# Dilated attention in a two-block kernel: exponentials by each key set's own maximum, weighed together at the division

## What is computed

```python
for q, k, v, off in zip(qs, ks, vs, offs):          # three sets
    s = einsum('bqhd,bqkhd->bhqk', qi, kg) * scale  # masked: -inf outside
    lse = logsumexp(s); p = exp(s - lse)
    outs.append(einsum('bhqk,bqkhd->bqhd', p, vg)); lses.append(lse)
wts = softmax(stack(lses), axis=0)
return sum(wts * stack(outs), axis=0)
```

## Time and profile before

| | |
|---|---|
| median of 3 runs | 1580.39 us (1578.71 to 1582.65) |
| the profiled execution's own time | 1575.34 us |
| its span in the trace | 1573.4 us |
| TensorE busy | 1500.6 us (95%) |
| VectorE busy | 924.0 us (59%) |
| ScalarE busy | 627.8 us (40%) |
| granted TensorE clock, mean | 0.974 of full speed |

### The profile page before, as it was taken

The page is one execution under the profiler, slowest core; times in us unless marked ns, Lnnn a source line. Parts: engine busy times, 40 slices in busy tenths (PEclk is TensorE's granted clock), DMA queues, the critical chain, the costliest instruction groups (busy, mean ns, idle before and its releaser), DMA issues.

```text
span 1573.4 us, 20863 instructions
## 1 busy us (share of the span) xinstructions
PE 1500.6 (95%) x8538; PEld 1112.7 (71%) x8538; DVE 924.0 (59%) x1573; ACT 627.8 (40%) x1018; POOL 39.8 (3%) x39
## 2 busy tenths in 40 slices
PE   7999999998999999998799999999999999999998
PEld 6876343336988534433678778989987877889897
DVE  4975111118896411112998778988868856765555
ACT  6442111114333211112554655444445556454443
POOL 0000000000000000000400000000001000000000
PEclk9999999998999999999899999999999999999999
DMA  9877999995564999999646243998935522435540
GB/s 358 315 308 304 411 421 421 422 421 223 205 269 170 402 410 420 422 421 419 227 164 241 108 149 148 351 344 320 361 117 195 193 96 83 159 136 186 188 161 27
DMA packets 58777, 420.77 MB, mean 267 GB/s; under 512 B 6625, under 2 KB 6689, under 8 KB 8370
## 3 DMA queue, kind: packets, MB, share of 16 engines
q1 hardware_dynamic: 58034, 417.19, 68.0%
q0 software_dynamic: 640, 2.14, 0.4%
HBM read 418.26 MB, written 1.05 MB: 266 GB/s over the span
## 4 chain that ended last, share of the span: by engine, by line
PE 80%; DVE 12%; ACT 6%; DMA 1%; issue 1%; SPq 0%; DVEq 0%; ACTq 0%
PE ps L758 77%; DVE lo L1874 3%; ACT AR L1775 3%; DVE AR L1867 2%; PE ps L844 1%; DMA raw<-in_moe 1%; ACT hi L1444 1%; DVE ACC L1867 1%; DVE AR L1864 1%; PE ps L1328 1%; PE ps L1067 1%; PE ps L1302 1%; ACT AR L1787 0%; DVE TINY L1867 0%; DVE TINY L1864 0%
## 5 line engine op out<-in xcount | busy, mean ns | idle before, releaser
L1874 DVE TENSOR_TENSOR lo<-raw,hi 128x1024 fp32r<-128x1024 f32 x300 | 367.3, 1246 | 106.4 <-ACT hi L1444 105.4
L1444 ACT ACTIVATE hi<-raw 128x1024 fp32r<-128x1024 f32 x300 | 310.4, 1056 | 194.7 <-PE ps L758 189.3
L758 PE MATMUL ps<-T,hi 128*128 128x256 f32 x1792 | 333.1, 287 | 8.8 <-DVE lo L1874 8.5
L758 PEld LDWEIGHTS ps<-T,hi 128*128 128x128 f32 x1792 | 284.5, 194 | 20.2 <-DVE lo L1874 9.3
L758 PE MATMUL ps<-hi,T 128*128 128x512 f32 x896 | 286.7, 396 | 3.9 <-DVE T L1867 3.0
L758 PE MATMUL ps<-T,lo 128*128 128x256 f32 x896 | 255.2, 285 | 0.0
L758 PEld LDWEIGHTS ps<-hi,T 128*128 128x128 f32 x896 | 169.9, 190 | 40.7 <-issue 5.7
L758 PE MATMUL ps<-lo,T 128*128 128x512 f32 x448 | 175.6, 392 | 0.0
L758 PEld LDWEIGHTS ps<-T,lo 128*128 128x128 f32 x896 | 173.5, 194 | 0.0
L758 PE MATMUL ps<-hi,AF 128*128 128x512 f32 x512 | 166.1, 396 | 0.5 <-DVE AF L2593 0.5
L1867 DVE SCALAR_TENSOR_TENSOR AR<-AR,ps 128x512 f32<-128x512 f32 x52 | 35.6, 686 | 179.6 <-ACT AR L1605 110.9
(11 more groups left out here) (234 smaller groups left out, 1819.8 us busy)
## 6 DMA issues: line engine op xcount, KB each, us to landing
raw<-in_moe SPq DMA_DIRECT2D x76, 1024.0 KB, 16.7
raw<-in_b_ff SPq DMA_DIRECT2D x64, 1024.0 KB, 5.1
AR<-in_moe SPq DMA_DIRECT2D x60, 1024.0 KB, 15.4
raw<-in_ada SPq DMA_DIRECT2D x48, 1024.0 KB, 6.6
ring<-in_moe SPq DMA_DIRECT2D x44, 1024.0 KB, 15.8
raw<-in_b_in SPq DMA_DIRECT2D x24, 1024.0 KB, 6.5
raw<-in_b_gate SPq DMA_DIRECT2D x16, 1024.0 KB, 4.8
ACC<-in_moe SPq DMA_DIRECT2D x12, 1024.0 KB, 18.5
```

Source lines behind the costliest of these rows:

```text
L758: return e.matmul(o, l, r, start=a, stop=z, skip_group_check=True)
L1444: e.activation(hi[n % NC][:, :], raw[place[c]][:, 1024 * half:1024 * half + 1024], ACT.Copy).then_inc(*to("hi", "hi", n))
L1874: tt(lo[n % NC][:, :], r, hi[n % NC][:, :], SUB).then_inc(*to("lo", "lo", n))
```

## The change

Each b set now gets its own exponentials by its own maximum as soon as that is known. After the third set VectorE takes the largest of the three maxima and each set's distance to it (`off`, six numbers for a query row); ScalarE turns these into weights (`part`). At the division VectorE multiplies sums by weights, adds, takes the reciprocal and multiplies weights by it, and each set is scaled by its own factor. The division becomes a job of its own, "soft", that is yielded with the score job of the next pair; after the last pair it takes a yield of its own, so that what follows it (probs 7 onward) moves by one yield: value 6 comes after `bb` tile 1 instead of tile 0, value 7 after tile 2, value 8 after tile 3, ahead of value 9.

```diff
             if j < PAIRS:
-                yield [("score", j)]
+                yield [("score", j)] + ([("soft", j - 1)] if j else [])
+            elif j == PAIRS:
+                yield [("soft", j - 1)]
...
+        def soft_mem(i):
+            return tuple(tiny(f"b_{x}{i % 4}", 6) for x in ("le", "of", "pa", "sm"))
...  ScalarE, job "score"
                             i, n, of, _, _, _, g = SETS[j]
-                            if n < of - 1:
-                                continue
-                            mx, sm = tiny(f"b_mx{i % 2}", 8), tiny(f"b_sm{i % 2}", 8)
-                            w.wait_ge(*after("max", l, i))
-                            for k in range(of):
-                                jj = j - 2 * (of - 1 - k)
-                                [waits for probs jj - 8, or for qk_turn]
-                                for q in range(2):
-                                    [exp of PB[jj % 8][:, q, :], bias mx[:, q], sum to sm[:, 2 + 2 * k + q]]
+                            less, off, part, sm = soft_mem(i)
+                            if n == 2:
+                                w.wait_ge(*after("off", l, i))
+                                e.activation(part, off, ACT.Exp, scale=m.SC).then_inc(*to("tile_out", "part", l, i))
+                            w.wait_ge(*after("max", l, j))
+                            [waits for probs j - 8, or for qk_turn]
+                            for q in range(2):
+                                [exp of PB[j % 8][:, q, :], bias less[:, 2 * n + q], sum to sm[:, 2 * n + q]]
...  VectorE, largest(j)
-                        if n < 2:
-                            return
-                        w.wait_ge(*last("step"))
-                        e.tensor_reduce(mx[:, 0:2], mx[:, 2:8].rearrange("p (g q) -> p q g", q=2), AX.X, MAX).then_inc(*to("step"))
                     w.wait_ge(*last("step"))
-                    ts(mx[:, 0:2], mx[:, 0:2], -m.SC, None, MUL, NOP).then_inc(*to("step", "max", l, i))
+                    ts(less[:, x], most[:, x], -m.SC, None, MUL, NOP).then_inc(*to("step", "max", l, j))
+                    if n == 2:
+                        e.tensor_reduce(most[:, 6:8], most[:, 0:6].rearrange("p (g q) -> p q g", q=2), AX.X, MAX).then_inc(*to("step"))
+                        w.wait_ge(*last("step"))
+                        tt(off.rearrange("p (g q) -> p g q", q=2), most[:, 0:6].rearrange("p (g q) -> p g q", q=2),
+                           most[:, 6:8].unsqueeze(1).broadcast_to([128, 3, 2]), SUB).then_inc(*to("step", "off", l, i))
...  VectorE, divided(j), b heads
-                        e.tensor_reduce(sm[:, 0:2], sm[:, 2:8].rearrange("p (g q) -> p q g", q=2), AX.X, ADD).then_inc(*to("step"))
-                        w.wait_ge(*last("step"))
-                        e.reciprocal(sm[:, 0:2], sm[:, 0:2]).then_inc(*to("step"))
+                        w.wait_ge(*after("part", l, i))
+                        tt(by, sm, part, MUL).then_inc(*to("step"))
+                        w.wait_ge(*last("step"))
+                        e.tensor_reduce(total[:, 0:2], by.rearrange("p (g q) -> p q g", q=2), AX.X, ADD).then_inc(*to("step"))
+                        w.wait_ge(*last("step"))
+                        e.reciprocal(total[:, 2:4], total[:, 0:2]).then_inc(*to("step"))
+                        w.wait_ge(*last("step"))
+                        tt(by.rearrange("p (g q) -> p g q", q=2), part.rearrange("p (g q) -> p g q", q=2),
+                           total[:, 2:4].unsqueeze(1).broadcast_to([128, 3, 2]), MUL).then_inc(*to("step"))
                     w.wait_ge(*last("step"))
                     for k in range(of):
                         jj = j - 2 * (of - 1 - k)
                         for q in range(2):
-                            o = m.PB[jj % 8][:, q, :]
-                            ins = ts(o, o, sm[:, q:q + 1], None, MUL, NOP)
+                            o, x = m.PB[jj % 8][:, q, :], 2 * k + q
+                            ins = ts(o, o, by[:, x:x + 1], None, MUL, NOP)
...  VectorE, the walk
                     elif what == "score":
                         for j in (2 * a[0], 2 * a[0] + 1):
                             largest(j)
+                    elif what == "soft":
                         for j in (2 * a[0], 2 * a[0] + 1):
                             divided(j)
```

More of the change, by code:

```diff
@@ L1761, in attention @@
                             i, n, of, _, _, _, g = SETS[j]
-                            if n < of - 1:
-                                continue
-                            mx, sm = tiny(f"b_mx{i % 2}", 8), tiny(f"b_sm{i % 2}", 8)
-                            w.wait_ge(*after("max", l, i))
-                            for k in range(of):
-                                jj = j - 2 * (of - 1 - k)
[L1768 to L1771, removed]
-                                for q in range(2):
-                                    o = m.PB[jj % 8][:, q, :]
-                                    src = PS[bank["score", l, j]][:, 256 * q:256 * q + 256] if g is None else o
-                                    ins = e.activation(o, src, ACT.Exp, scale=m.SC, bias=mx[:, q:q + 1],
-                                                       accum_out=sm[:, 2 + 2 * k + q:3 + 2 * k + q])
+                            less, off, part, sm = soft_mem(i)
@@ new lines, in attention @@
+                            if n == 2:
+                                w.wait_ge(*after("off", l, i))
+                                e.activation(part, off, ACT.Exp, scale=m.SC).then_inc(*to("tile_out", "part", l, i))
+                            w.wait_ge(*after("max", l, j))
+                            if j > 7:
+                                w.wait_ge(*after("probs", l, j - 8))
+                            else:
+                                w.wait_ge(*after("qk_turn", l, 5, 0))
+                            for q in range(2):
+                                o, x = m.PB[j % 8][:, q, :], 2 * n + q
+                                src = PS[bank["score", l, j]][:, 256 * q:256 * q + 256] if g is None else o
+                                ins = e.activation(o, src, ACT.Exp, scale=m.SC, bias=less[:, x:x + 1], accum_out=sm[:, x:x + 1])
@@ L1777, in attention @@
                             if g is None:
                                 ins.then_inc(*to("tile_out", "score_out", l, j))
-                                also(("exp", l, i), ("score_out", l, j))
+                                also(("exp", l, j), ("score_out", l, j))
                             else:
-                                ins.then_inc(*to("tile_out", "exp", l, i))
+                                ins.then_inc(*to("tile_out", "exp", l, j))
                     elif what == "probs":
@@ L2457, in largest @@
                 def largest(j):
-                    i, n, of, qp, kp, _, g = SETS[j]
-                    mx = tiny(f"b_mx{i % 2}", 8)
+                    i, n, of, _, _, _, g = SETS[j]
+                    most, x = tiny(f"b_mx{i % 4}", 8), slice(2 * n, 2 * n + 2)
+                    less, off, _, _ = soft_mem(i)
                     pb, p = m.PB[j % 8], PS[bank["score", l, j]]
@@ L2463, in largest @@
                     if g is None:
-                        e.tensor_reduce(mx[:, 0:2], p[:, :].rearrange("p (q k) -> p q k", q=2), AX.X, MAX).then_inc(*to("step"))
+                        e.tensor_reduce(most[:, 0:2], p[:, :].rearrange("p (q k) -> p q k", q=2), AX.X, MAX).then_inc(*to("step"))
                     else:
@@ L2473, in largest @@
                                                          m.MK[:, g, 256 * q:256 * q + 256], 1.0, -3e38, ADD, MAX,
-                                                         mx[:, 2 + 2 * n + q:3 + 2 * n + q])
+                                                         most[:, 2 * n + q:2 * n + q + 1])
                         ins.then_inc(*to("step", "score_out", l, j))
-                        if n < 2:
-                            return
+                    w.wait_ge(*last("step"))
+                    ts(less[:, x], most[:, x], -m.SC, None, MUL, NOP).then_inc(*to("step", "max", l, j))
+                    if n == 2:
+                        e.tensor_reduce(most[:, 6:8], most[:, 0:6].rearrange("p (g q) -> p q g", q=2), AX.X, MAX).then_inc(*to("step"))
                         w.wait_ge(*last("step"))
-                        e.tensor_reduce(mx[:, 0:2], mx[:, 2:8].rearrange("p (g q) -> p q g", q=2), AX.X, MAX).then_inc(*to("step"))
-                    w.wait_ge(*last("step"))
-                    ts(mx[:, 0:2], mx[:, 0:2], -m.SC, None, MUL, NOP).then_inc(*to("step", "max", l, i))
+                        tt(off.rearrange("p (g q) -> p g q", q=2), most[:, 0:6].rearrange("p (g q) -> p g q", q=2),
+                           most[:, 6:8].unsqueeze(1).broadcast_to([128, 3, 2]), SUB).then_inc(*to("step", "off", l, i))
                 def divided(j):
@@ L2486, in divided @@
                         return
-                    sm = tiny(f"b_sm{i % 2}", 8)
```

(12 more changed lines are left out.)

## The result

The changed kernel takes 1590.27 us in the median of 9 runs (1587.40 to 1597.21), the kernel before beside it 1581.22 (1576.77 to 1586.58, 9 runs). The ratio is 1.0064, with a 95% interval of 1.0047 to 1.0081: about 10.1 us slower, by the ends 7.4 to 12.8. Forecast were +6.4 us, 1586.8 us, and 1582 to 1591. The direction and the places were as forecast, and the median lies within the forecast range; the loss itself was underpriced, by 2.7 us by the medians and 3.7 by the ratio. What follows finds the rest in TensorE's clock: about half of the loss is waiting and about half is work at half clock.

The account below looks back on a forecast made before the run. TensorE was taken as the bound (80% of the span), so only its stalls counted: 2.2 + 5.8 - 1.6 = +6.4 us, clock 0, on 1580.39 gave 1586.8 us. The range for 8 in 10 was 1582.0 to 1591.0.

Parts of the forecast that it names:

- Place A: At probs 0 and 1, divisions ready later for TensorE: 0.5 us lost in layer 0, 1.7 in layer 1, +2.2.
- Place B: Before probs 3, second b division queued behind `lo` and score 6's maxima: new stall, 2.9 us a layer, +5.8.
- Place C: At the first `bb` tile, work arrives 0.8 us earlier; stall falls from 3.48 to 2.7, -1.6 for two layers.
- Prices: Trace-based costs: small instructions 0.20 us apart with a wait, 0.07 without; division chain 0.8; `part` 0.2, bounds 0 to 0.5.
- The queue ledger of 6.4 us: Sum over the three places in both layers: 2.2 + 5.8 - 1.6 = +6.4 us.
- The rule of the Trainium skill: Chained VectorE instructions cost the same with and without a semaphore; as a rival +2.5 us, 1582.9, chance 0.05.
- Clock: TensorE's half-speed stretches after stalls, some 1.6 us each: gain and loss counted equal, 0, ends -3.2 and +3.2.
- The low rival: No slow stretch after the `bb` 0 stall or the new one before probs 3: +3.2 us, 1583.6; chance 0.20.
- The "not slower" rival: Exponentials alone held the division at probs 0; maxima and late `lo` fit idle time: -7.5 us, 1572.9; chance 0.06.
- The dearer rival: Low clock at all three places and `part` at its upper bound: +10.8 us, 1591.2; chance 0.10.

Follow-up runs that it names:

- the filled kernels: The kernel before and the changed kernel, each with throw-away transposes filling TensorE's stalls; 1574.71 us and 1578.98 us.
- own_same_job: Changed kernel with each division back in the job of its own pair and without the last division's extra yield; 1579.14 us, ratio 0.9991.
- delay_only: Kernel before with only the divisions a pair later, maxima still joint and exponentials where they were; 1597.38 us, ratio 1.0094.
- after_again: The changed kernel run once more, unchanged; 1591.83 us, ratio 1.0067.
- heads_filled: Like own_same_filled, with 16, 3 and 20 filling transposes and the first set of both heads multiplied first; 1576.78 us, ratio 0.9973.
- own_same_filled: own_same_job with filling transposes: 16 before tile 0's, 13 before tile 1's, 24 before the first `bb` matmul; 1572.82 us, ratio 0.9952.
- after_filled: Changed kernel with throw-away transposes before tiles 0, 1, 6, 7 and `bb` 0 (26, 6, 4, 10, 18); 1578.98 us, ratio 0.9979.

## Why the prediction was right and wrong

**Right.** *Place A*, 0.5 and 1.7 us: from score 0 to the transposes of tile 1 the filled kernels differ by 0.6 us in layer 0 and 1.8 in layer 1. Late `hi` behind early exponentials showed as `lo` waiting for ScalarE, 0.16 us in layer 0 where `ada` covers it. *Place B*, 2.9 a layer: 0.84 and 1.65, taken away by own_same_job, made larger by delay_only. That the user of the division doesn't move with it was the main term, and it is shown. *Place C*, -0.8 a layer: 3.48 to 2.71. *Prices*: small waiting instructions 0.20 apart, chain 0.79, `part` 0.21. The queue ledger of 6.4 us came out as 2.6 and 3.9 up to `bb` 0 with the clock held. The rule of the Trainium skill ("VectorE: DVE Perf Modes", The DRAIN you can't avoid) on semaphores between chained instructions, which would have given +2.5, doesn't hold for instructions of 2 to 6 numbers a partition in the rows before and after: they start 0.20 apart with a wait and 0.07 without, and four with waits take 0.79.

**Wrong.** The step that failed is **Clock**, "So I count the gain and the loss as equal, 0." The term was about +6 as a sum of lost time, and about +5 net of what hides in the stalls. Busy time at half clock loses half of itself (2.88 x 0.5 = 1.4 over 868 to 871). Added up in this way over the windows, the profiled execution before loses 3.3 us behind A and 3.2 behind C, 6.5 in all. The one after loses 5.9 behind A (3.7 and 2.2 in the two layers), 4.8 behind B (1.7 and 3.1) and 1.7 behind C, 12.4 in all. So A gave +2.7 where the prediction had 0. B gave +4.8, of which it had allowed for 3.2 at most, and C gave -1.5, where it had hoped for up to -3.2. In the second execution, after_again, the sum is 13.3. The fillers give the two numbers another way: 5.9 and 11.3 us are won back. Two things had been missed. The low stretch behind A was longer, 6.8 or 10.2 us in all four layers profiled and not 3.4. The longer stall there may be the cause, but delay_only, whose gaps in layer 0 are those of the kernel before, had 6.8 behind them in that layer too, so what sets the length stays open. And B's two short gaps, 0.84 and 1.65 with 0.6 of transposes between, were followed by a fall in both layers of both profiles; I had taken them as half a chance.

The two parts don't simply add to 6.4 + 6. In the two profiled executions the idle gaps at the three places grew from 15.7 to 20.6 us, 4.9, since tile 0's transposes at half clock fill 0.46 of the gap behind them in each layer. With the clock's 6.0 and the 0.9 that the shifted yield brought back (the prediction had it at 0), the attention takes 10.0 us longer from score 0 to `F` (5.5 and 4.6). The spans differ by 14.9; the other 4.9 lie outside the attention, most of it in low stretches near 1175 and 1210 us that were longer or not there before. The medians differ by 9.1, since the clock costs each execution something else.

The low rival ("the low clock leaves C and stays away from B") was half right at C, in one layer of one execution, and wrong at B. The "not slower" rival fell at the order in VectorE's queue, as put: the 2.05 us of waiting for exponentials went, and more than as much was queued in their place. The dearer rival, 1591.2, with low clock at all three places, is nearest to what happened; I gave it 0.10. It is near by luck in part: it has `part` at 0.5 where it took 0.21, and nothing for the longer stretch behind A. That the median fell inside the range of the forecast is no merit of the clock term either.

## What to carry to other kernels

Moving a step later in an in-order queue gives its producer time only if its consumer moves too; otherwise list what now stands in front of it, with the waits that these things bring along. When TensorE is the bound and stalls for a few microseconds, price the stall at its length plus the slow stretch behind it, which here about doubled the cost. Some throw-away transposes inside the wait won the clock back in the three kernels that were timed without and with them (5.9, 11.3 and 6.3 us); with them the kernel before is still faster than the changed one, by 4.3 us, so they don't rescue the change. Early work for one engine is not free when it stands ahead of what another engine waits for.

## What was not expected of the hardware

Two idle gaps of 0.84 and 1.65 us, split by 0.63 us of transposes, were followed by a fall to 1.2 GHz in all four layers profiled, while a single gap of 2.7 (C) was followed by one in three of the same four layers. In heads_filled a wait of 1.91 us, some microseconds behind gaps of 0.52 and 0.34, was followed by a fall in both layers, and one of 0.86 in own_same_filled by none. Waiting TensorE kept busy with transposes of no use ran on at 2.4 GHz, but for one stretch of 3.4 us in after_filled, and the kernel before won 5.9 us by 54 such transposes a layer. The trace can't say whether the same holds on several cores; it wasn't tried.
